# A gate chunk between two latent chunks, one conditioning sum moved to another chunk, and a half-way mean made by another engine

## The reference

```python
def rms_norm(x, g):
    y = xf * lax.rsqrt(jnp.mean(xf * xf, axis=-1, keepdims=True) + EPS)
    return (y * g)

def modulate(x, g_pre, shift, scale):
    return rms_norm(x, g_pre) * (1 + scale) + shift

def residual_add(x, y, g_post, gate, res_w):
    return x + res_w * (1 + gate) * rms_norm(y, g_post)

def token_mixer(hn, ...):
    proj = hn @ w_in                      # three of the outputs: moba_qkv, sb_qkv, latents
    y_a = moba_attention(...)             # 8 heads
    y_b = stick_breaking_attention(...)   # 8 heads
    qc = rms_norm(c_q, q_norm) @ w_uq     # 8 latent heads: queries from a latent of 256,
    kv = rms_norm(c_kv, kv_norm) @ w_ukv  # keys and values from a latent of 128
    y_c = causal_softmax_attention(...)
    g = sigmoid(gates + b_gate)           # 3 x 1024 gate columns
    return sum over branches of (y @ w_branch) * g, times w_out

# conditioning: mod = silu(c) @ ada_w + ada_b gives every shift, scale and gate
```

## Time and profile before

| | before |
|---|---|
| time, median of 3 runs | 1729.32 us (1728.82 to 1733.48) |
| the profiled execution | 1728.25 us |
| its span, first to last instruction | 1726.5 us |
| TensorE products busy | 1670.9 us, 12368 products |
| VectorE busy | 1259.0 us, 1815 instructions |
| ScalarE busy | 877.2 us, 1241 instructions |
| mean granted TensorE clock | 0.996 |
| moved by DMA | 398.92 MB, mean 231 GB/s |

### The profile page before, as it was taken

The page is one execution under the profiler, slowest core; times in us unless marked ns, Lnnn a source line. Parts: engine busy times, 40 slices in busy tenths (PEclk is TensorE's granted clock), DMA queues, the critical chain, the costliest instruction groups (busy, mean ns, idle before and its releaser), DMA issues.

```text
span 1726.5 us, 29665 instructions
## 1 busy us (share of the span) xinstructions
PE 1670.9 (97%) x12368; PEld 1555.2 (90%) x12368; DVE 1259.0 (73%) x1815; ACT 877.2 (51%) x1241; POOL 21.9 (1%) x39
## 2 busy tenths in 40 slices
PE   3999999998999999999999999999999999999998
PEld 3999989987999889989989997999889989989996
DVE  7777879987777666676878775778666676878553
ACT  4555466654544365665463435543365665463432
POOL 0000000000000000000000000000000000000000
PEclk9999999999999999999999999999999999999999
DMA  9879746786677944746548786677745846547552
GB/s 385 327 255 257 258 165 223 197 311 268 244 279 277 291 169 181 225 156 232 205 149 294 283 231 240 241 277 279 292 165 181 224 162 230 201 150 263 193 171 112
DMA packets 71077, 398.92 MB, mean 231 GB/s; under 512 B 8224, under 2 KB 8736, under 8 KB 36256
## 3 DMA queue, kind: packets, MB, share of 16 engines
q1 hardware_dynamic: 67968, 387.56, 63.9%
q0 software_dynamic: 2976, 9.47, 1.6%
HBM read 395.92 MB, written 1.08 MB: 230 GB/s over the span
## 4 chain that ended last, share of the span: by engine, by line
PE 84%; DVE 5%; ACT 4%; DVEq 2%; DMA 2%; issue 1%; ACTq 1%; SPq 1%
PE att L649 18%; PE lin L472 18%; PE lin L473 18%; PE lin L474 18%; PE att L752 2%; DVE lo L1284 2%; ACT hi L901 2%; PE lin L512 2%; PE lin L514 2%; PE lin L522 1%; PE att L804 1%; DVEq L1639 1%; DMA ada_s<-in_ada 1%; PE pt L781 1%; DMA ada_w<-in_ada 1%
## 5 line engine op out<-in xcount | busy, mean ns | idle before, releaser
L1284 DVE TENSOR_TENSOR lo<-raw,hi 128x2048 fp32r<-128x2048 f32 x262 | 600.1, 2291 | 278.6 <-ACT hi L901 278.0
L472 PE MATMUL lin<-h_hi,hi 128*128 128x256 f32 x2448 | 689.6, 282 | 3.6 <-DVE ra L1540 2.6
L473 PE MATMUL lin<-h_lo,hi 128*128 128x256 f32 x2448 | 683.3, 279 | 0.0
L474 PE MATMUL lin<-h_hi,lo 128*128 128x256 f32 x2448 | 683.2, 279 | 0.0
L901 ACT ACTIVATE hi<-raw 128x2048 fp32r<-128x2048 f32 x262 | 500.6, 1911 | 190.6 <-PE att L649 116.9
L472 PEld LDWEIGHTS lin<-h_hi,hi 128*128 128x128 f32 x2448 | 460.1, 188 | 7.3 <-issue 7.2
L473 PEld LDWEIGHTS lin<-h_lo,hi 128*128 128x128 f32 x2448 | 460.2, 188 | 1.5 <-issue 1.4
L474 PEld LDWEIGHTS lin<-h_hi,lo 128*128 128x128 f32 x2448 | 460.1, 188 | 0.0
L1300 DVE CUSTOM_DVE_ANT_0 ada_w<-ada_w,cs 128x1024 f32<-128x1024 f32 x179 | 217.8, 1219 | 14.8 <-DMA ada_w<-in_ada 14.7
L1137 ACT ACTIVATE work<-lin 128x256 f32<-128x256 f32 x88 | 33.9, 386 | 280.0 <-PE lin L474 271.8
L649 PE MATMUL att<-hi,act_lo 128*128 128x512 f32 x440 | 135.5, 389 | 0.0
(11 more groups left out here) (299 smaller groups left out, 2061.2 us busy)
## 6 DMA issues: line engine op xcount, KB each, us to landing
raw<-in_w SPq DMA_DIRECT2D x269, 1024.0 KB, 4.9
ada_w<-in_ada SPq DMA_DIRECT2D x179, 512.0 KB, 5.3
ada_s<-in_ada SPq DMA_DIRECT2D x13, 512.0 KB, 15.2
bias<-in_bias POOLq DMA_DIRECT2D x16, 256.0 KB, 4.2
ffn_row<-rows POOLq DMA_DIRECT2D x5, 512.0 KB, 9.6
x<-in_x SPq DMA_DIRECT2D x1, 1024.0 KB, 9.7
dcon<-in_dcon SPq DMA_DIRECT2D x1, 1024.0 KB, 7.6
ra<-rows POOLq DMA_DIRECT2D x2, 512.0 KB, 5.3
```

Source lines behind the costliest of these rows:

```text
L472: mm(out, w_hi, a_hi, start=start, stop=False, skip_group_check=skip)
L473: mm(out, w_hi, a_lo, start=False, stop=False, skip_group_check=skip)
L474: return mm(out, w_lo, a_hi, start=False, stop=stop, skip_group_check=skip)
L1284: tt(lo[c % SPLIT][:], raw[:, c % RAW, :], hi[c % SPLIT][:].bitcast(F32), ALU.subtract).then_inc(*s_lo.up(c))
```

## The change

It has three parts.

1. `gate.3` stands between `uq` and `ukv` in the order of the mixing stage, in both layers. ScalarE's takes of `ukv` move from step 14 to 15; VectorE's follow the chunk by themselves.
2. One conditioning sum moves from after `o.out.1` to after the last branch chunk of the first block (position 25 in `ADA_AT`). The loads of later rows follow from the same list.
3. The half-way value (mean of squares of the first half, plus eps) is made by VectorE. ScalarE's squares are scaled so that their sum is already a mean; it signals after the first square and waits for VectorE's value before `root`. The tile of these values holds one column for x beside the two for the result.

```diff
-             + [f"gate.{k}" for k in range(3)] + ["uq", "ukv"] + [f"gate.{k}" for k in range(3, 12)]
+             + [f"gate.{k}" for k in range(3)] + ["uq", "gate.3", "ukv"] + [f"gate.{k}" for k in range(4, 12)]
...
-    at += list(range(4, 21)) + [20, 20, 21, 22, 24]
-    at += [AT["o.out.0"] + 2 + i // 2 for i in range(4)]
+    at += list(range(4, 21)) + [20, 20, 21, 22, 24, 25]
+    at += [AT["o.out.0"] + 2 + i // 2 for i in range(3)]
...
-                act(factor[:, a:a + 1], total[:, a, total_at:total_at + 1], ACT.Ln, bias=rest, scale=1.0 / D)
+                act(factor[:, a:a + 1], total[:, a, total_at:total_at + 1], ACT.Ln, bias=rest)
...
-            def half_done(a):
-                nc.scalar.drain()
-                act(total_of_half[:, a:a + 1], total[:, a, 0:1], ACT.Identity, bias=eps[:, 0:1], scale=1.0 / D)
+            def squares(out, of, a, at):
+
+                return act(out, of, ACT.Square, scale=D ** -0.5, accum_out=total[:, a, at:at + 1])
...
-                act(work[2 * a], att[:, 2 * a, :], ACT.Square, accum_out=total[:, a, 0:1]).then_inc(
-                    *s_squared.up((tag, a)))
-                half_done(a)
+                squares(work[2 * a], att[:, 2 * a, :], a, 0).then_inc(*s_squared.up((tag, a)))
                 eng.wait_ge(*s_z.at((tag, a)))
-                act(work[2 * a + 1], att[:, 2 * a + 1, :], ACT.Square, accum_out=total[:, a, 1:2])
+                squares(work[2 * a + 1], att[:, 2 * a + 1, :], a, 1)
+                eng.wait_ge(*s_half_mean.at((tag, a)))
                 root(tag, a, 1, total_of_half[:, a:a + 1])
...
                 for half in range(2):
                     eng.wait_ge(*s_x.at((by, 1, half)))
-                    act(work[2 + half], x[:, 1, half * 512:(half + 1) * 512], ACT.Square,
-                        accum_out=total[:, 1, half:half + 1])
+                    ins = squares(work[2 + half], x[:, 1, half * 512:(half + 1) * 512], 1, half)
                     if half == 0:
-                        half_done(1)
-                root(tag, 1, 1, total_of_half[:, 1:2])
+                        ins.then_inc(*s_x_squared.up(tag))
+                eng.wait_ge(*s_half_mean.at((tag, "x")))
+                root(tag, 1, 1, total_of_half[:, 2:3])
...
-                    13: [lambda: take_latent_q(l, 0)], 14: [lambda: take_latent_k(l, 0), lambda: take_latent_k(l, 1)],
+                    13: [lambda: take_latent_q(l, 0)], 15: [lambda: take_latent_k(l, 0), lambda: take_latent_k(l, 1)],
...
+            def half_of_result(tag, a):
+
+                ts(total_of_half[:, a:a + 1], total[:, a, 0:1], EPS, None, ALU.add).then_inc(*s_half_mean.up((tag, a)))
+
+            def half_of_x(tag):
+                eng.wait_ge(*s_x_squared.at(tag))
+                ts(total_of_half[:, 2:3], total[:, 1, 0:1], EPS, None, ALU.add).then_inc(*s_half_mean.up((tag, "x")))
...
                 if normed and n == 0:
                     eng.wait_ge(*s_squared.at((tag, a)))
+                    half_of_result(tag, a)
...
+                half_of_x(pre)
                 split_half(c, 1)
                 scaled_x(pre, buf, 1)
...
             plus("down", flat_f, 1, False)
+            half_of_x("norm3")
             split_half(c, 0)
             scaled_x("0.pre0", flat_f, 0)
             final_norm(1)
+            half_of_x("0.pre0")
             split_half(c, 1)
             scaled_x("0.pre0", flat_f, 1)
```

More of the change, by code:

```diff
@@ L197, in program @@
         total = sb("total", [P, 2, 2])
-        total_of_half = sb("total_of_half", [P, 2])
+        total_of_half = sb("total_of_half", [P, 4])
         factor = sb("factor", [P, 2])
@@ L265, in program @@
         s_hi, s_taken_a, s_silu = signal("hi"), signal("taken_a"), signal("silu")
+        s_x_squared = signal("x_squared")
         s_squared, s_r, s_h_hi, s_part_a = signal("squared"), signal("r"), signal("h_hi"), signal("part_a")
@@ L276, in program @@
         s_z, s_scaled, s_h_hi_v = signal("z"), signal("scaled"), signal("h_hi_v")
-        s_glu = signal("glu")
+        s_glu, s_half_mean = signal("glu"), signal("half_mean")
         s_act, s_taps, s_merged, s_rot, s_lat = (signal("act_made"), signal("taps"), signal("merged"), signal("rot"),
@@ L941, in factor_of_x @@
                     eng.wait_ge(*s_x.at((by, 0)))
-                    act(two(by_token(work_all)[:, 0, :]), two(x[:, 0, :]), ACT.Square, accum_out=total[:, 0, 0:1])
+                    squares(two(by_token(work_all)[:, 0, :]), two(x[:, 0, :]), 0, 0)
                     root(tag, 0, 0, eps[:, 0:1])
@@ L1150, in _ @@
             for a in range(2):
-                act(att[:, 2:4, :], two(x[:, a, :]), ACT.Square, accum_out=total[:, a, 0:1])
+                squares(att[:, 2:4, :], two(x[:, a, :]), a, 0)
                 root("norm1", a, 0, eps[:, 0:1])
```

## The result

The kernel after takes 1721.72 us (median of 4 runs, 1720.76 to 1722.67) where the kernel before, run beside it, takes 1731.40 (4 runs, 1728.82 to 1733.93): a ratio of 0.9944 with a 95% interval of 0.9924 to 0.9964, so 9.7 us less, 6 to 13. The forecast was 8.6 less and 1720.5. A second measurement of the same two kernels gave 1719.91 (5 runs) against 1730.25 (9 runs), 0.9940 (0.9928 to 0.9953). One further execution of before, in another set of 32, took 1850.11 us at a mean granted clock of 0.852 and stands in no comparison here.

What follows compares the result with a forecast made beforehand. TensorE, busy 1670.9 of 1726.5 us, was taken as the bound. Terms -4.8 - 2.4 - 1.7 - 0.2 + 0.5 = -8.6 gave 1719.65 from the profiled 1728.25, 1720.7 from the median; forecast 1720.5, range 1718.0 to 1724.0.

Steps and rivals of the forecast that it cites:

- The latents, -4.8: Mixing stage, gate.3 between uq and ukv: both TensorE waits go, 2.4 us less per layer, bounds 1.2 and 2.8.
- Rival B: Mixing stage: the latent wait is moved, gate.4 waits for VectorE's copies; 1.1 us gained per layer, 1722.7 us; chance 0.12.
- Rival D: Mixing stage: ScalarE and VectorE don't overlap with ukv in step 15, so the kernel is slower, 1735.9 us; chance 0.03.
- `out`, -2.4: First block's output stage: VectorE's result 1.0 us earlier and the clock does not fall; 2.4 us less, bounds 0 and 3.0.
- Rival A: Output stage keeps its slow clock, or reordering VectorE's queue gives nothing: 0 to 1.0 us gained, 1722.5 us; chance 0.19.
- Five stage ends, -1.7: Stage ends with a residual: second square of x follows 0.35 us sooner at each; 1.7 us less, bounds 1.0 and 2.8.
- Rival C: Stage ends: ScalarE's saving is swallowed, as the root or second square of x waits for VectorE; 1722.2 us; chance 0.09.
- The kernel's end, -0.2: End of the kernel, where the result's squares are last: 0.2 us less, bounds 0 to 0.3.
- `down`, +0.5: First block's down stage: VectorE's split waits for ScalarE's first square, first transposes later; 0.5 us more, bounds 0.2 to 0.8.
- shift whole: Convolution stage and the DMA-heavy down stage behind out: they start from TensorE's progress and move by the whole gain.
- The sum, -8.6: Whole kernel: all terms together bring 8.6 us less, 1719.65 from the profiled execution, 1720.7 from the median; forecast 1720.5 us.
- A and B together: Slow output clock and moved latent wait both happening: 1724.9 us, within 0.3% of no change; no separate chance given.

Runs made afterwards that it cites:

- e1_gate: The kernel before with only gate.3 moved between uq and ukv: 1726.66 us (median of 10) against 1730.69, ratio 0.9973.
- e2_sum: The kernel before with only one conditioning sum moved to the last branch chunk of the first block: 1727.51 us (median of 10), ratio 0.9983.
- e3_mean: The kernel before with only the half-way mean made by VectorE: 1729.54 us (median of 10), ratio 0.9997.
- e6_before: The kernel before again, unaltered, for a second profile: 1732.02 us for the one execution, with a span of 1730.2.
- e11_before_fill: The kernel before with 22 and 4 fillers instead of 8 and 8 at the first block's down stage: 1727.19 us (11 runs), ratio 0.9985.
- e10_fill18: e8_best with 18 fillers instead of 22 ahead of the first transposes of down: 1717.60 us (5 runs), ratio 0.9929 to before.
- e7_order: The kernel after with VectorE's half-way value for norm3 made behind the first half split at down: 1719.48 us (5 runs), ratio 0.9936 to before.
- e8_best: e7_order with 22 and 4 fillers instead of 8 and 8 at the first block's down stage: 1715.37 us (4 runs), ratio 0.9912 to before.
- e4_fill: The kernel before with 11 instead of 5 filler groups ahead of the first block's out transposes: 1729.46 us (median of 10), ratio 0.9996.

## Why the prediction was right, step by step

- **The latents, -4.8.** Measured 2.6 and 2.4 in the two layers of the profile, 2.7 and 2.6 in `e1_gate`, -4.7 by its time. Counted from the end of `uq`, the steps came out within 0.3 us: the exponential done at 2.6 (749.81) where 2.7 was forecast, the scores at 11.0 (758.19) where 11.3 was, `gate.4` at 13.8 where 13.9 was, and the copy just in time. Rival B (a wait for VectorE's copies) did not happen. Rival D (no overlap in step 15) did not either: ScalarE was through with the gate's take and in its split (754.11) before TensorE started `ukv`.
- **`out`, -2.4.** Measured -2.6, as 1.15 of earlier work and 1.5 of clock, -2.9 by the time of `e2_sum`. VectorE's part was forecast at 1.0 and the two pauses went where the prediction put them. That 1.0 holds for one execution: it counts 0.66 for the last row's wait, which is 0.50 to 1.35 in the six profiles without the move, and the pause at `out` is longer where this wait is. The reason given for the clock (1.7 lies nearer to 1.3 than to 2.7) is right in outcome and too simple as a rule: a pause of 2.6 to 3.5 at this place lost the clock in four traces (before, `e3_mean`, `e6_before`, `e11_before_fill`) and 3.31 kept it in one, while 1.6 to 1.7 kept it in all seven traces that have it. At `down` 2.03 lost it (`e10_fill18`), which lies nearer to 1.7 than to 2.7. So the clock held in every trace with part 2, as forecast, but the comparison that it rests on was weaker than it looked. The term is 1.5 to 1.7 in an execution where before falls, and nothing where it does not; how often that is, the traces do not tell. Rival A did not happen.
- **Five stage ends, -1.7.** Measured 0.40 in four and 0.5 in one, 2.1 in all, where 0.35 each was taken. Counted from the first filler of `0.out`, the second square of the result starts 0.25 earlier than before (0.92 for 1.17), the first square of x 0.11 earlier (3.22 for 3.33), the second square of x 0.42 earlier (3.88 for 4.30), and the scaling 0.40 earlier. So between the squares of x the gain was 0.31, not 0.35, and of the result's squares, counted at nothing, 0.11 came through; the rest of their 0.25 was lost since VectorE's product became the later one, as the text said. Rival C did not happen.
- **The kernel's end, -0.2.** Measured -0.25, from the last product to the end.
- **`down`, +0.5.** Measured +0.48 by VectorE's two starts, and shown by `e7_order`. What the prediction missed is the stage around it: VectorE's result also came 0.22 later behind the first filler than in before (6.59 for 6.37), and 0.2 had been lost ahead of the fillers, so that of the 2.6 won at `out` 0.9 was gone at the second transposes of `down`. The forecast that the DMA-heavy stages "shift whole" does not hold to the tenth: VectorE waits there for conditioning rows, and with the same code at this place the time from filler to inputs was 8.6 to 10.1 us in six profiles and 8.7 to 10.5 in four. The row's wait accounts for it to within 0.1, as shown above: without it the 0.69 between after and before (10.16 and 9.47) is 0.46, the new wait, and 0.23 of a later row. The wait was forecast near 6.4 and was 6.6.
- **The sum, -8.6.** The second profile of after has a span of 1717.9, 8.6 below that of the first profile of before, with all feed-forward products at the same rate in both. That it meets the forecast to the tenth is luck: at the second transposes of `down` it is only 1.0 ahead, where the steps have 1.9, and behind them it gains 7.6, where they have 6.7. The first profile shows only -5.6, since three of its feed-forward stages ran at the slower rate; at the marks of TensorE up to `0.out` it stands within 0.3 of where the steps put it (-4.65 there), and loses 1.1 to 1.2 in each of those three. The time, 1721.72 for 1720.5, is close for two reasons that work against each other: the gain was 9.7 (10.3 in the second measurement) and not 8.6, and before took 1731.40 beside it and not the 1729.32 from which the forecast starts.
- **A and B together.** By the prediction's own prices (2.0 and 2.2 on 1720.5) they come to 1724.7, not 1724.9. The forecast doesn't rest on it.

The Trainium skill (TensorE: Matmul & The Clock Gate, "What's actually happening") had it that where the level changes differs from run to run; with the long pause that loses the clock in four traces and keeps it in one, the runs agree in the outcome and do not show its cause.

## What to carry to other kernels

Where one engine is busy all the time, the list of its waits is the list of what a change can bring; each wait priced from the two timelines around it came out within half a microsecond. A wait for data read from one trace is one draw of several: the same code waited 0.50 to 1.35 us for a row at `out`, so look for it in a second profile before you price it. When a pause is shortened, look at the clock behind it as well, since in this case it was worth more than the pause, and covering the pause with cheap products (`e8_best`) took more than reordering the work that caused it. A gain of 2 us in 1730 is read from the stages of a trace, and from the times only after ten runs or more, if at all.

## What the runs showed of the hardware

**Products have two rates.** In a stretch of uninterrupted work 48 products of 256 columns take either 5.60 or 5.65 us, at a granted clock of 1.00 both times. ScalarE's take of each chunk's result in the second feed-forward stage of layer 0 shows it, first in the first profile of after, then in the second profile of the same kernel:

```profile
1159.69 0.39 ACT L1137 ACTIVATE work<-lin 128x256 f32<-128x256 f32 x1 [3.46 <-PE lin L475]
1165.34 0.39 ACT L1137 ACTIVATE work<-lin 128x256 f32<-128x256 f32 x1 [3.46 <-PE lin L475]
```

```profile
1158.29 0.39 ACT L1137 ACTIVATE work<-lin 128x256 f32<-128x256 f32 x1 [3.41 <-PE lin L475]
1163.89 0.39 ACT L1137 ACTIVATE work<-lin 128x256 f32<-128x256 f32 x1 [3.41 <-PE lin L475]
```

The rate holds for all 19 chunk distances of a stage and differs between stages. Of four such stages in each profile, before has none at 5.65 and two in its second profile; after three and none; `e8_best` three; `e11_before_fill` two; `e4_fill` one; the others none. It costs 1.0 us per stage by the chunk distances (19 x 0.053) and 1.1 to 1.2 over the whole stage in after, so some 4 us if all four are slow, where the times of before spread over 6.4 us (31 runs). Two profiles of the same code differ in it, before as well as after, so the code does not fix it; what sets it is open.

**The clock's fall is not set by the length of the pause before it alone.** A pause of 3.31 us at `out` kept 2.4 GHz (`e1_gate`), one of 2.61 us there lost it (`e3_mean`), and so did one of 2.03 us at `down` (`e10_fill18`), while 1.61 to 1.72 at `out` kept it seven times. How long the lower level lasts differs too: at `down` the sixteen fillers behind the first transposes took 4.57 and 4.85 us in the two profiles of after and 5.67 in `e7_order`.
